# Expert rows gathered by selection products, 13 landing slots, low weight parts written in place

## The reference, cut to what matters

```python
def swiglu(x, w_gate, w_up, w_down):
    return (jax.nn.silu(x @ w_gate) * (x @ w_up)) @ w_down

# moe_swiglu, D_MODEL = 1024, D_FF = 2816, N_EXPERTS = 8, TOP_K = 2
logits = (xt @ router_w).astype(jnp.float32) + router_b.astype(jnp.float32)
top_logit, top_e = lax.top_k(logits, TOP_K)
gate = jax.nn.softmax(top_logit, axis=-1)
# every token's normalised row goes through its two experts, is scaled by
# their gates and is added to the token's row
```

## Time and profile before

| | us |
|---|---|
| median of 3 executions (1436.23 to 1436.75) | 1436.52 |
| the profiled execution | 1437.85 |
| its span, first to last instruction | 1436.0 |
| TensorE busy (modelled ends), share of the span | 1384.0, 96% |
| VectorE busy | 893.0, 62% |
| ScalarE busy | 697.5, 49% |
| expert part, from its first load to the end | 699 to 1436 |

### The profile page before, as it was taken

How to read it: one execution, slowest core, us unless ns; L and a number is a source line. 1 busy time by engine, 2 the same in 40 slices (tenths; PEclk the granted TensorE clock), 3 DMA queues, 4 the chain that set the end, 5 groups by cost and what they waited for, 6 DMA issues and landing times.

```text
span 1436.0 us, 19041 instructions
## 1 busy us (share of the span) xinstructions
PE 1384.0 (96%) x7514; PEld 1059.8 (74%) x7514; DVE 893.0 (62%) x1026; ACT 697.5 (49%) x771; POOL 58.3 (4%) x99
## 2 busy tenths in 40 slices
PE   9999999999999999999989999899999999999996
PEld 8898888888888889888867766566665665666675
DVE  6788977555545778897687545444444453445487
ACT  6347644544445336663576434433345343345374
POOL 2000000000000000000210000000000000000002
PEclk9999999999999999999999999999999999999999
DMA  8545554455454644554779999999999999999994
GB/s 339 208 149 182 191 184 176 148 212 198 179 200 172 214 164 166 188 183 165 279 293 353 402 420 422 409 422 420 422 408 421 421 421 421 420 421 421 421 420 159
DMA packets 79423, 424.20 MB, mean 295 GB/s; under 512 B 9248, under 2 KB 9424, under 8 KB 45536
## 3 DMA queue, kind: packets, MB, share of 16 engines
q1 hardware_dynamic: 72864, 402.16, 70.6%
q0 software_dynamic: 6048, 20.15, 4.2%
q10 hardware_dynamic: 416, 0.60, 0.1%
HBM read 414.48 MB, written 8.39 MB: 294 GB/s over the span
## 4 chain that ended last, share of the span: by engine, by line
PE 72%; DMA 18%; DVE 4%; ACT 3%; issue 2%; SPq 0%; POOL 0%; DVEq 0%; POOLq 0%
PE ps L909 22%; DMA late<-experts_dram 14%; PE ps L1462 9%; PE ps L1208 8%; PE ps L1414 5%; PE ps L886 5%; PE ps L1472 5%; PE ps L897 5%; DMA raw_m<-experts_dram 4%; PE ps L1185 4%; DVE w_lo L2153 2%; PE ps L1425 1%; ACT w_hi L1654 1%; ACT w_hi_x L1654 1%; DVE w_lo_x L2153 1%
## 5 line engine op out<-in xcount | busy, mean ns | idle before, releaser
L2013 DVE TENSOR_TENSOR w_lo<-raw_m,w_hi 128x2048 fp32r<-128x2048 f32 x113 | 257.7, 2288 | 111.3 <-ACT w_hi L1580 111.3
L1580 ACT CAST w_hi<-raw_m 128x2048 fp32r<-128x2048 f32 x113 | 214.6, 1906 | 126.3 <-PE ps L909 56.2
L2153 DVE TENSOR_TENSOR w_lo<-late,w_hi 128x2048 fp32r<-128x2048 f32 x59 | 135.0, 2289 | 97.2 <-ACT w_hi L1654 97.0
L909 PE MATMUL ps<-w_hi,hT_hi 128*128 128x512 f32 x464 | 183.1, 395 | 0.0
L909 PE MATMUL ps<-w_hi,hT_lo 128*128 128x512 f32 x464 | 180.9, 390 | 0.0
L909 PE MATMUL ps<-w_lo,hT_hi 128*128 128x512 f32 x464 | 180.7, 389 | 0.0
L1654 ACT CAST w_hi<-late 128x2048 fp32r<-128x2048 f32 x59 | 112.4, 1905 | 79.9 <-DMA late<-experts_dram 77.6
L1462 PE MATMUL ps<-w_hi,hT_hi 128*128 128x512 f32 x268 | 112.9, 421 | 19.2 <-DVE w_lo L2153 18.2
L2153 DVE TENSOR_TENSOR w_lo<-raw_m,w_hi 128x2048 fp32r<-128x2048 f32 x40 | 91.6, 2289 | 44.0 <-ACT w_hi L1654 44.0
L1414 PE MATMUL ps<-late,light_x 128*64 128x256 f32 x896 | 109.6, 385 | 0.0
L1462 PE MATMUL ps<-w_lo,hT_hi 128*128 128x512 f32 x268 | 107.3, 400 | 0.0
(11 more groups left out here) (428 smaller groups left out, 2538.0 us busy)
## 6 DMA issues: line engine op xcount, KB each, us to landing
late<-experts_dram SPq DMA_DIRECT2D x165, 1024.0 KB, 14.4
raw_m<-dense_dram SPq DMA_DIRECT2D x226, 512.0 KB, 4.1
raw_m<-experts_dram SPq DMA_DIRECT2D x99, 1024.0 KB, 14.0
bias<-b_in_dram POOLq DMA_DIRECT2D x26, 256.0 KB, 5.8
late<-dense_dram SPq DMA_DIRECT2D x4, 512.0 KB, 9.8
raw_m<-front_dram SPq DMA_DIRECT2D x4, 384.0 KB, 4.5
raw_m<-front_dram SPq DMA_DIRECT2D x2, 768.0 KB, 7.3
x_rows<-prow POOLq DMA_DIRECT2D x3, 512.0 KB, 10.9
```

Source lines behind the costliest of these rows:

```text
L909: ins = mm(ps[:, b, :], hT[a][:, k, t * P:(t + 1) * P], wsp[r][:, s, kk * W:(kk + 1) * W], start=(k == 0 and pa == 0), stop=(k == KT - 1 a ...
L1580: copy(w_hi[:, g % RS, :], slot_raw(g, False)).then_inc(hi_ready, 1)
L2013: tt(w_lo[:, g % RS, :], slot_raw(g, False), w_hi[:, g % RS, :], ALU.subtract)\
L2153: tt(lo_slot(j), slot_raw(m, True), hi_slot(j), ALU.subtract).then_inc(lo_ready, 1)
```

## The change

- **Landing slots.** `RE` goes from 8 to 13: three in `raw_m`, seven in `late`, and three in the memory of `w_lo`. The low part of a heavy chunk is now written over the chunk where it landed (`lo_slot(n)` is the landing slot), so the ring `w_lo`, `w_lo_x` and `xs` go.
- **When a slot is free.** `raw_free(n)` waits for TensorE's use of chunk n - 13, heavy or light (`chunk_used`). The first 13 wait as before: slots 0 to 2 for the last dense chunks' splits, 3 to 9 for `merged_ready`, 10 to 12 for TensorE's use of the last three dense chunks.
- **Rows.** `x_rows` with its zeros, scatters and reads is gone, and ScalarE's scaled rows with it. VectorE builds each slot's selection (`select_slot`, two comparisons) some chunks before it is needed, from `pos_mid` (`order_rows`, at m = 2). TensorE collects the rows of slots 1 to 7 with `rows_of`, in the place of the transposes: 32 products a slot, of 128 columns for a heavy and 64 for a light one.
- **Order of VectorE's work.** `order_experts()` moves from ahead of `split_moe(0, 2)` to m = 0, behind `split_moe(0, 3)`, with one copy more; `count_picks()` moves to m = 9, `rows_of_picks()` to m = 15. Slot 7's selection is built with the others and no longer at its second down chunk.
- **Schedule.** `LEAD` goes from 5 to 4, so 11 heavy chunks come ahead of the first light one, and a heavy step more lies between light ones.
- **Picked rows.** The four indirect reads of `y_rows` go into the landing slots of the first two chunks of slot 7 among the last 13, once these are used, and none waits for an addition.

```diff
-    RM, RE, RS, RX = 3, 8, 3, 4
+    RM, RE, RS, RX = 3, 13, 3, 4
...
-    LEAD, TAIL = 5, 5
-    BETWEEN = ((0, 1, 2, 3, 5, 6, 7, 9, 10), (0, 2, 3, 5, 6, 7, 9, 10)) * 2
+    LEAD, TAIL = 4, 5
+    BETWEEN = ((0, 1, 2, 3, 5, 6, 7, 9, 10),) * 3 + ((0, 2, 3, 5, 6, 7, 9, 10),)
...
+        def lo_slot(n):
+
+            s = n % RE
+            if s < RM:
+                return raw_lo[:, s, :]
+            return late_lo[:, (s - RM) * CK:(s - RM + 1) * CK] if s < RE - RS else w_lo[:, s - (RE - RS), :]
...
+        def raw_free(n):
+
+            if n < RM:
+                return lo_ready, MOE_BASE + n - RM + 1
+            if n < RE - RS:
+                return merged_ready, L * NT
+            if n < RE:
+                return last_use(MOE_BASE - RE + n)
+            return chunk_used(n - RE)
...
-            for s in range(1, E):
-                n = LC if s in LIGHT else P
-                pool.dma_start(x_rows[s * T:s * T + n, :], prow[0:n, :]).then_inc(x_zeroed, 16)
...
-                    pool.indirect_dma_start(out=x_rows, out_offset=bass.IndirectOffsetOnAxis(ap=row_x[:, j:j + 1], axis=0),
-                                            in_=xs[:, t, :], in_offset=None).then_inc(x_stored, 16)
...
             for j in range(2 * NT):
-                if j == 3:
-                    pool.wait_ge(rows_added, 1)
+                if j % 2 == 0:
+                    pool.wait_ge(*chunk_used(PICK_CHUNKS[j // 2]))
...
+            def rows_of(b, k, at_col, n, x, first, last):
+
+                for lo in range(2):
+                    for t in range(NT):
+                        ins = mm(ps[:, b, at_col:at_col + n], (xn_hi, xn_lo)[lo][:, t, k * P:(k + 1) * P],
+                                 sel(t, x)[:, 0:n], start=(first and lo == t == 0), stop=(last and lo == t == 1),
+                                 skip_group_check=True)
+                return ins
...
-                tt(lo_slot(j), slot_raw(m, True), hi_slot(j), ALU.subtract).then_inc(lo_ready, 1)
+                tt(lo_slot(n), slot_raw(n, True), hi_slot(j), ALU.subtract).then_inc(lo_ready, 1)
...
-                order_experts()
                 split_moe(0, 2)
...
                     if m == 0:
+                        order_experts()
+                    if m == 2:
+                        order_rows()
+                    if m in SELECT_AT:
+                        select_slot(SELECT_AT[m])
+                    if m == 9:
+                        count_picks()
+                    if m == 15:
                         rows_of_picks()
```

More of the change, by code:

```diff
@@ L172, in program @@
         LGATHER_AT[AT[s, "gu", 0, 0] - 2 if s == LIGHT[0] else AT[s - 1, "gu", NF - 1, 1] + 1] = s
+    SELECT_AT = {m + 4: s for m, s in LGATHER_AT.items() if s != LIGHT[-1]}
+    SELECT_AT = {m: s + 1 for m, s in SELECT_AT.items()}
+    for m, (s, half) in HGATHER_AT.items():
+        if half and s != HEAVY[-1]:
+            SELECT_AT[m + 5] = HEAVY[HEAVY.index(s) + 1]
+    SELECT_AT[5], SELECT_AT[7] = LIGHT[0], HEAVY[1]
+    PICK_CHUNKS = [m for m in range(len(MS0) - RE, len(MS0)) if MS0[m][0] == E - 1][:2]
     SLICE = {}
@@ L201, in selections @@
     def selections(pas, e):
-        return 3 + e // 2 if pas else 1 + (e > 0)
+        return 2 + e // 2 if pas else 1
     def gate_turn(pas, e):
@@ L286, in program @@
                 USED.append(use)
+            CHUNK_USED.append(use)
     ctx = ExitStack()
@@ L345, in program @@
         xn_lo = over("xn_lo", [P, NT, D], tmp_at)
[L346 to L348 removed]
+        w_hi_x = over("w_hi_x", [P, CK], late_at + 4 * 7 * CK)
+        raw_lo = over("raw_m_lo", [P, RM, CK], raw_at)
+        late_lo = over("late_lo", [P, 7 * CK], late_at)
+        raw_x = nc.alloc_sbuf_tensor_at("raw_x", [P, RS, CK], f32, offset=w_lo_at)
         idg = over("idg", [P, NT, P + 2], bias_at)
@@ L415, in picked @@
         def picked(j):
-            return prow[:, :] if j == 2 else xs[:, j % 2 if j < 2 else 0, :]
+            n, h = PICK_CHUNKS[j // 2], j % 2
+            return slot_raw(n, True)[:, h * D:(h + 1) * D]
         def sel(t, x):
@@ L478, in slot_raw @@
                 return (gates_flat, mqk_flat)[n - RM + 1]
-            s = n % (RE if moe else RM)
-            return raw_m[:, s, :] if s < RM else late[:, (s - RM) * CK:(s - RM + 1) * CK]
+            if not moe:
+                return raw_m[:, n % RM, :]
+            s = n % RE
+            if s < RM:
+                return raw_m[:, s, :]
+            return late[:, (s - RM) * CK:(s - RM + 1) * CK] if s < RE - RS else raw_x[:, s - (RE - RS), :]
+        def lo_slot(n):
+            s = n % RE
+            if s < RM:
+                return raw_lo[:, s, :]
+            return late_lo[:, (s - RM) * CK:(s - RM + 1) * CK] if s < RE - RS else w_lo[:, s - (RE - RS), :]
         def hi_slot(j):
             return w_hi[:, j % RX, :] if j % RX < RS else w_hi_x[:, :]
-        def lo_slot(j):
-            return w_lo[:, j % RX, :] if j % RX < RS else w_lo_x[:, :]
         ps = ctx.enter_context(nc.psum_tensor("ps", [P, 8, W], f32))
@@ L804, in _ @@
                             .then_inc(y_out_l, 16)
-            for tag, g in (("gather1", HEAVY[-1]), ("gather", LIGHT[-1])):
-                b, k = FILL[(0, g), tag, 0]
-                pool.wait_ge(full[b], k + 1)
             pool.wait_ge(zero_in, 16)
@@ L2555, in gates_of_picks, with select_slot @@
                 settle()
+            def select_slot(s):
+                n, x = (LC, 0) if s in LIGHT else (P, 1)
+                ready = sel_light if s in LIGHT else sel_heavy
+                for t in range(NT):
+                    which = pos[:, t, E - 1:E] if s == E - 1 else pos_mid[:, t, s - 1:s]
+                    tt(sel(t, x)[:, 0:n], iota[:, 0:n], which.to_broadcast([P, n]), ALU.is_equal).then_inc(ready, 1)
             def select(c, both):
```

126 lines of the change are left out of this document (42 added, 84 removed).

## The result

| | before | changed |
|---|---|---|
| median of 4 runs each, same chip | 1436.63 us (1436.23 to 1437.09) | 1420.24 us (1418.17 to 1420.56) |
| ratio to before, 95% | 1 | 0.988 (0.9867 to 0.9894) |
| profiled execution / its span | 1437.85 / 1436.0 | 1420.02 / 1418.2 |
| bytes moved in the whole kernel | 424.20 MB | 416.87 MB |
| TensorE's last down product ends | 1422.67 us | 1405.66 us |

The kernel is 1.2% faster, and 7.2 us slower than the forecast of 1413. The 7.33 MB that the page shows fewer are the row store's 7.34.

A forecast was written before the change was run, and what follows sets the result against it. Weight loads bound the expert part, TensorE second. After the change TensorE ends at 1400, 22.7 us earlier, plus 0.8 at the end: 23.5 off 1437.85 gives 1414.3, less 1.3 for the median: 1413, range 1411 to 1418 (0.58).

The forecast's parts named there:

- TensorE's path: First expert chunk to last down product: steps 632 us, products 24.9 us, wait and clock; ends at 1400 instead of 1422.7.
- the clock: Lowered TensorE clock behind its wait at the start of the expert part: perhaps 3 us.
- the products: TensorE's 224 row-selection products for slots 1 to 7, at 0.111 us each: 24.9 us, 17.8 at the low end.
- The long wait: TensorE's early wait of 6 us, until VectorE split chunk 4 and multiplied the hidden rows; 4.5 us of it stays.
- The DMA path: Stream of weight loads through the expert part: gains 25 us, 17.4 of row store and 7.6 of idle; ends at 1397.7.
- The row store's 17.4 us: Zeros, scatters and reads back that go: 7.34 MB, 17.4 us of the DMA engines at 421 GB/s.
- The order: Expert order SP needs before chunk 11, the first light one: ready at 744.7, that chunk's load flowing from 747.
- Does holding a slot until TensorE's use choke it? No: At 748 five of thirteen slots are free; eight heavy chunks cost one slot in 23 us, then slots come back.
- B: Rival: TensorE becomes the bound and selection products cost more, 0.14 to 0.18 us each; 1420 to 1428; chance 0.15.
- C: Rival: SP's wait for the expert order lasts 6 to 12 us longer, costing its length; 1419 to 1425; chance 0.12.
- D: Rival: slower than before, products at a 512-column product's price or lower clock; about 1439, or 1450 to 1470; chance 0.05.
- E: Rival: light products at 0.056 us take 7 us off TensorE, so DMA decides; 1405 to 1411; chance 0.10.

The follow-up runs named there:

- lazy: Order first, with SP reading each of the six order values only before the first load that needs it; 1418.59 us.
- five ahead: Changed kernel with LEAD = 5 and the old order of slots between, so 14 heavy chunks precede the first light one; 1420.03 us.
- Order first: Changed kernel with order_experts() back ahead of split_moe(0, 2), as in the kernel before; 1417.81 us.

## Why the prediction was right, and where its 7 us are

**The direction and the mechanism** hold, and the number is near, partly because two late paths still came out level. TensorE ends 1422.67 - 1405.66 = 17.0 us earlier, where the sum had 22.7. The two paths come out nearly level, as summed: less work for TensorE brings 2.3 us, bytes put back cost 14.6.

**The 7.2 us** are two terms. 5.7 of them are TensorE's path, which ends at 1405.66 instead of 1400. The other 1.5 are in how the sum was turned into a median: it took off the 1.3 by which the profiled execution of the kernel before lay above its median, while in the changed kernel the profiled execution (1420.02) lies 0.2 below it. That part is chance.

**TensorE's path**, summed to 1400, has one mis-sized term, the clock. From the first chunk to the last down product it took 670.1 us, where the sum had 664.6. *The work*, steps and products together, is 657.1 for 656.9. In it *the products* took 26.1 us, 0.117 each, for 24.9, some 0.5 of it at the lower clock. The choice of the upper bound for 64 columns was right: 0.109 measured, not 0.056. The Trainium skill (TensorE: Matmul & The Clock Gate, "LDWEIGHTS") says that a weight load takes its columns over 1.2 GHz, which is 107 ns for 128. By that rule, the trace agrees: 0.109 us a product with 64 moving columns, and 0.108 to 0.119 in the blocks with 128. *The long wait* is 3.92 for 4.5, and 0.5 us of waits for weights come on top. *The clock* cost 8.6 us (the estimate above, from 18.6 us of work at the lower level) for 3. It had been counted behind the long wait alone; it fell again at the light gathers of 768.65, 909.4 and 1205.1, not at the one of 1057.0. The first of these falls, at 770 to 775, granted 0.75:

```profile
770.00:775.00 5.00, 5.00 (x29) 4.38 (x29) 0.69 (x1) 0.23 (x1) 0.00 (x0) 0.75 1.01 419
```

The same step stands in the reading of the kernel before. Its clock was put at 3.6 us, from the stretch of 745 to 790 alone; over the whole path TensorE worked 18.5 us at the lower level there too, 8.6 us by the same estimate. Its waits for split weights were 30.4 us and not the 40 that were left over. That was the room, and the changed kernel used all of it but 0.5. (Two of the prediction's sums are off in their last digit: 713 x 405 makes 288.8, and 735.44 + 637 makes 1372.4.)

Of the changed kernel's 8.6 us of clock some 3.9 lie before 800 us, near the 3 summed, and 4.8 behind. By the table the second part alone would mostly have come back as waits, since the stream was no earlier: TensorE stood still for it at 1347. The forecast had said "few waits of TensorE for weights", and so it is.

**The DMA path**, summed to 1397.7, comes out at 1405.6, level with TensorE's. Term by term:
- *The row store's 17.4 us* are right in bytes (416.87 for 424.20 MB) and about right in price (14.6 for the same bytes put back).
- *The order* was ready at 744.6 (744.7 said), so the steps on VectorE were summed well. The six value reads were taken as 0.5 of at most 2 us, and 2 us with issue and start; from the start of the order's last step to the first light load, 748.28, are 3.9, and the engines flow from 750, not 747: 3 us.

```profile
744.39 0.17 DVE L2484 CAST bias<-bias 128x6 int32<-128x6 f32 x1
```

- *"Does holding a slot until TensorE's use choke it? No"* is the step that failed. The check counted free slots at 748 and the mean pace after it, 2.8 against 2.49 us a chunk. But the five free slots are asked for within three us, at 748.28 and 749.21, and from then to 800 SP waits 16 times for TensorE, whose heavy chunks are slower than the loads. The dent from 775 to 795 costs (421 - 388) x 20 = 0.66 MB, 1.6 us, and 419 instead of 421 to 1000 another 1. The runs make it larger than these 2.6: the slots decide also what an early start is worth (earlier loads in lazy and in five ahead brought nothing), and with ten and eight of them TensorE waits 7.1 and 14.6 us longer for its weights.
- *The last landing*, from SP's last issue at 1369.94 and its 24.6 us to the landing, was at 1394.5 instead of 1387: 3 for the start, 2.6 for the slots, and the 2 left go to the picks, behind 1385, where the engines fell to 366 and 298 GB/s. These picks had been costed at full pace. To the last down product are 11.1 us, 10.7 before. Yet TensorE doesn't wait for that landing. Its last wait for weights ends at 1347.26, and in the tail its heavy steps, 2.8 us a chunk, last longer than the loads: there the stream's path ends at the tail's first chunks.

**The subtraction in place** takes what the other form did, and **the end** gained its 0.8 us (12.5 us from TensorE's end to the span's for 13.3); the last two additions run without a wait:

```profile
738.23 2.29 DVE L2141 TENSOR_TENSOR raw_m_lo<-raw_m,w_hi 128x2048 fp32r<-128x2048 f32 x1 [1.11 <-ACT w_hi L1648]
...
1402.40 2.67 DVE L2531 SCALAR_TENSOR_TENSOR xt<-late,bias,xt 128x1024 f32<-128x1024 f32 x2
```

**The rivals.** The time, 1420.24, lies in the ranges of both B and C, and neither is what happened. C has its first step: the order's wait is indeed longer than summed, but it doesn't cost its length one to one. A first light load 5.3 us earlier came with 2.4 us, and with an earlier TensorE; another 2.7 us of it brought nothing. B is right that TensorE's path is no longer behind the stream's, but dearer products have 1.2 of the 7.2 us at most. D and E are out at 0.117. What did it, the stream tied to TensorE's first 100 us by the slots and a clock that fell more often, was in no rival.

**What stays open.** A kernel with the row store and thirteen slots wasn't tried, so the slots' worth was only measured without the store; nor were thirteen slots that come free at the split, with the low part elsewhere, for which there is no room beside them. No run changed the clock alone, so its 8.6 us, and what of them reached the end, are read from traces and not shown by an experiment. Why it falls wasn't settled. Order first has the same block of 32 products of 64 columns, from 767.0 to 770.5, and the clock stayed at 1.00 from 765 to 780, and at 1.00 from 910 to 925, where the changed kernel was granted 0.77. The kernel before, without these products, was at the lower level near 905 and 1205 too (0.72 and 0.69 over 5 us).

## What to carry to other kernels

Before a ring's slots are held longer, count at the end of its worst stretch how many landed chunks may wait unused: that number, not the free slots at one moment, is the stream's lead, and a stall filled ahead of that point comes back behind it. What the lead is worth is read from the consumer's waits: here they were 15.1 us with 8 slots, 7.6 with 10 and 0.5 with 13, and the times followed (1435.7, 1427.8, 1420.5). Once they are near zero, neither more slots nor an earlier load alone can bring anything. Where both paths come out level in the sum, write the consumer's time as work, waits and clock for each run: what is saved in one term and comes back in another is then seen at once.

## What the hardware showed that I had not expected

- Six value reads of SP, one after the other, and the issue behind them took 3.9 us, counted from the start of the order's last step (744.39 to 748.28; 739.09 to 742.96 with order first); one read and the issue took 1.1 (739.13 to 740.26).
- A selection product of 64 moving columns costs as much as one of 128: 0.109 and 0.111 us.
- After 32 such products in 3.49 us with no gap between them, the granted clock fell from the upper to the lower level for some 3 us. Before that, I had seen it fall only behind a wait. In order first the same block wasn't followed by a fall, so the block alone isn't the reason.
- Loads of 1 MB took 24 us in the median from issue to landing in the tail (21 to 26, issues from 1300 to 1375) and 13 to 14 over the whole expert part, while the pace was 421 GB/s from 1000 us on: a longer way to the landing doesn't mean a slower stream.
